# A two-layer diffusion backbone kernel: strides of 4192 and 4176 bytes for the weight slots, moving rows on multiples of 2048 bytes

## The chip, the core and the metric

The kernel runs on one core of a Trainium2 chip. The metric is device time in microseconds (us). TensorE (PE in the rows) multiplies, its weight loads have rows of their own (PEld), VectorE is DVE, ScalarE is ACT, GpSimd is POOL, and SyncE (SP) issues most of the DMAs. Times of single instructions are in nanoseconds (ns) where marked.

## What is computed

Two layers over 256 latent tokens and 256 context tokens, D_MODEL 1024, D_FF 2816, everything in float32. Cut to what matters:

```
for l in range(DEPTH):                                   # DEPTH = 2
    h  = h  + 0.5*m[2]*_swiglu(_modulate(_rms(h,  norm_w[l,0]), m[0], m[1]), ffn1_w_gu[l], ffn1_w_down[l])
    hc = hc + 0.5*mc[2]*_swiglu(...)                     # the same for the context
    u, uc = _modulate(_rms(h, norm_w[l,1]), ...), _modulate(_rms(hc, norm_w[l,1]), ...)
    y, yc = _hybrid_mixer(u, uc, ...)                    # differential attention | gated conv | pools, w_in, w_out
    h  = h + m[5]*y
    h  = h + 0.5*m[8]*_swiglu(_modulate(_rms(h, norm_w[l,2]), m[6], m[7]), ffn2_w_gu[l], ffn2_w_down[l])
    ...                                                  # the context too, except in the last layer
return h
```

m and mc are nine modulation vectors, silu(c) @ w_mod[l] + b_mod[l]. The weight matrices make up nearly all of the traffic and of the multiplications.

## The kernel before

**Three products for one.** The activations stand transposed in SBUF: 1024 features as 8 chunks of 128 partitions, 512 columns of tokens (the latent tokens first, then the context). Each float32 product x·w is made from a high and a low half of both: hi_w·hi_x + hi_w·lo_x + lo_w·hi_x. The helper `three` (lines 1167 to 1170) issues these as three float32r matmuls into one PSUM bank: L1168 has the weights' high half (whi) and the activations' high half, L1169 whi and the activations' low half, L1170 the weights' low half (wlo) and the activations' high half. Each matmul has its own weight load of 128 columns. The moving operand is a row of xh, xl (the layer's input) or ah, al (the hidden values of a feed-forward network) with 512 columns, 2048 bytes in a partition, or a half of such a row with 256 columns. In the value blocks of the mixer alone (192 matmuls) it is the other way round: the weights move and the activations are loaded.

**The weight stream.** The weights come in 320 blocks (NB) of 128 x 1024 float32, 8 tiles of 128 x 128, in the order of use. SP issues the DMA of block n into `raw[:, n % RING]`, RING = 5, when block n - 5 has been used (block_done). ACT copies it rounded into `whi[:, n % SPL]`, SPL = 4 (`split`, L398), when block n - 4 has been used. DVE subtracts: `wlo[:, n % RING] = raw - whi` (L685). wlo and raw are the same memory: the low half overwrites the raw block. PE waits for lo_done of block n, and the last matmul of a block counts block_done up. All queues are written out by hand; no scheduler orders them.

**Around it.** While the first feed-forward networks run, DVE also makes the modulation of later stages (L706, L710), a multiply-add of 128x512 at a time from `wm`, and PE sums it with small matmuls (L1229). The statistics of the norms (L1244, L1246, L1331), attention scores (L1371), values (L1403) and transposes are plain float32 matmuls, between the blocks.

**The layout.** Every SBUF tensor is placed behind the one allocated before it, on a multiple of 32 bytes. The first one starts at byte 16512 of each partition. The `hidden` and `wm0_place` stacks share the place of kq and what follows it. With the tensors' sizes this gives, for the ones that the float32r matmuls read:

```
tensor     starts at   start modulo 2048   step from slot to slot (or row to row)
wlo, raw   16512       128                 4096
whi        36992       128                 4096
xh         69760       128                 2048
xl         86144       128                 2048
ah         137344      128                 2048
al         182400      128                 2048
```

A tile of 128 weight columns has 512 bytes, so before the change every start address of a float32r matmul, weights or moving row, is 128 above a multiple of 512. A moving row of 512 columns runs from 128 to 2176 above a multiple of 2048; of its halves, the first runs from 128 to 1152 and the second from 1152 to 2176.

Of the kernel before, what the change touches and what calls it, by code (L numbers as in the profile page):

```python
# [22 lines left out]
F32, F32R = mybir.dt.float32, mybir.dt.float32r  # L23
# [3 lines left out]
P = 128  # L27
D = 1024
DC = D // P
S = 256  # L30
T = 2 * S
DEPTH = 2
# [11 lines left out]
TILES = 8  # L44
BLK = TILES * P
RING = 5
SPL = 4
GU = 2 * FC
DN = FC
HALF = DN // 2  # L50
# [6 lines left out]
TAIL_CHUNKS = (6, 7, 4, 5, 0, 1, 2, 3)  # L57
FFN = GU + DN
MIX = VB + QKB + CB + OB
# [4 lines left out]
HN = D // 2  # L64
# [5 lines left out]
START_UNITS = 4  # L70
UNIT_AT = {0: (4, GU // 4), 1: (16, GU // 4), 2: (27, 9)}
LATE_UNIT = 15
# [22 lines left out]
NCOL = _at  # L95
# [4 lines left out]
def program(nc, wstream, wmod, cols, x_t, out):  # L100
    with ExitStack() as ctx:
        def sb(name, shape, dt=F32):
            return ctx.enter_context(nc.sbuf_tensor(name, shape, dt))
# [2 lines left out]
            return ctx.enter_context(nc.semaphore(name))  # L106


        ring = ExitStack()
        raw = ring.enter_context(nc.sbuf_tensor("raw", [P, RING, BLK], F32))  # L110
        ring.close()
        wlo = sb("wlo", [P, RING, TILES, P], F32R)
        whi = sb("whi", [P, SPL, TILES, P], F32R)
        h = sb("h", [P, DC, T])
        xh = sb("xh", [P, DC, T], F32R)
        xl = sb("xl", [P, DC, T], F32R)
        xh32 = xh[:, :, :].bitcast(F32)
        wm = sb("wm", [P, 2, 2, HN])
        K = sb("K", [P, NCOL])
        cs = sb("cs", [P, DC * 2])  # L120
        modc = sb("modc", [P, DEPTH * N_MOD, DC, 2])
        acol = sb("acol", [P, DEPTH * 3, DC, 2])
        gcol = sb("gcol", [P, DEPTH * 3, DC, 2])
        lamc = sb("lamc", [P, DEPTH, 8])
        qws = sb("qws", [P, 16])
        mrows = sb("mrows", [P, P])

        shared_a = sb("shared_a", [P, 3 * T])
        macc = shared_a[:, 0:2 * HN].rearrange("p (v n) -> p v n", v=2)
        sq = shared_a[:, 0:2 * T].rearrange("p (a t) -> p a t", a=2)  # L130
        ssq = shared_a[:, 2 * T:3 * T]

        shared_b = sb("shared_b", [P, 4 * T])
        sil = shared_b[:, 0:2 * T].rearrange("p (a t) -> p a t", a=2)
        af = shared_b[:, 2 * T:4 * T].rearrange("p (a t) -> p a t", a=2)
        lnv = shared_b[:, 0:T]
        rstd = shared_b[:, T:2 * T]
        xt = shared_b[:, 2 * T:4 * T].rearrange("p (a t) -> p a t", a=4)
        hidden = ExitStack()
        ah = hidden.enter_context(nc.sbuf_tensor("ah", [P, FC * T], F32R))  # L140
        al = hidden.enter_context(nc.sbuf_tensor("al", [P, FC * T], F32R))
# [10 lines left out]
        sqk = sb("sqk", [P, 2, T])  # L152
        lnk = sb("lnk", [P, T])
        rq = sb("rq", [P, 2, T])
        shf = sb("shf", [P, S])
        rot = sb("rot", [P, S])
        prob = sb("prob", [P, 2, 2, T])
        att = sb("att", [P, 3, T])
# [7 lines left out]
        lsum = sb("lsum", [P, 2, 2, 2])  # L166
        linv = sb("linv", [P, 2, 2, 2])
        nlin = sb("nlin", [P, 2, 2])
        ps = ctx.enter_context(nc.psum_tensor("ps", [P, 8, T], F32))

        def col(name, i=0, n=1):
            a = COLS[name][0] + i
            assert i + n <= COLS[name][1]
            return K[:, a:a + n]

# [142 lines left out]
        @block.sync  # L318
        def _(sp):
            sp.dma_start(K[:, 0:EARLY], cols[:, 0:EARLY]).then_inc(cols_in, 16)  # L320
            sp.dma_start(h[:, :, :], x_t.rearrange("(c p) t -> p c t", p=P)).then_inc(x_in, 16)
            start_pairs = wmod[0:START_UNITS * PAIRS].rearrange("(u q) p n -> q p u n", q=PAIRS)
            for p in range(PAIRS - 1):
                sp.dma_start(wm0[:, p, :, :, :].rearrange("p u a n -> p u (a n)"), start_pairs[p])\  # L324
                    .then_inc(wm0_in[p], 16)
            for r in range(2):

                sp.dma_start(wm0[:, PAIRS - 1, :, r, :], start_pairs[PAIRS - 1][:, :, r * HN:(r + 1) * HN])\  # L328
                    .then_inc(wm0_in[PAIRS - 1 + r], 16)
            for n in range(NB):  # L330
                if n >= RING:

                    sp.wait_ge(block_done, n - RING + 1)
                sp.dma_start(raw[:, n % RING, :], wstream[n]).then_inc(raw_in[n % RING], 16)
                if n == 1:
                    sp.dma_start(K[:, EARLY:NCOL], cols[:, EARLY:NCOL]).then_inc(cols2_in, 16)
                    sp.dma_start(lamk[:, :], cols[:, NCOL:NCOL + NLAM]).then_inc(lam_in, 16)
            for d in range(DC):

                sp.wait_ge(h_done, h_count(5, d, 0))  # L340
                sp.dma_start(out[d * P:(d + 1) * P, :], h[:, d, 0:S]).then_inc(out_sem, 16)
            sp.wait_ge(out_sem, 16 * DC)
# [48 lines left out]
        def _(act):  # L391
            def split(n):

                act.wait_ge(raw_in[n % RING], 16 * (n // RING + 1))
                if n >= SPL:

                    act.wait_ge(block_done, n - SPL + 1)
                act.activation(whi[:, n % SPL, :, :].rearrange("p a b -> p (a b)"), raw[:, n % RING, :], ACT.Copy)\  # L398
                    .then_inc(hi_done, 1)

            def split_next(n):
                if n + SPL < NB:
                    split(n + SPL)

# [13 lines left out]
            def ffn(l, st):  # L418
# [11 lines left out]
                for b in range(HALF):  # L430
                    split_next(n0 + GU + b)
                if m + 1 < 6:
                    for d in range(JOINT):
                        square(m + 1, d)
                    ln_exp_tables()
                nd = n0 + GU + HALF
                for b in range(HALF - TAIL):
# [7 lines left out]
            def ln_exp_tables():  # L445

                act.preload_act_table_set("natural_log_exp_and_others")
# [225 lines left out]
        def _(dve):  # L673
            steps = [0]

            def own(ins):

                steps[0] += 1
                ins.then_inc(dve_step, 1)
                dve.wait_ge(dve_step, steps[0])  # L680
# [8 lines left out]
            def split_next(n):  # L689
                if n + SPL < NB:  # L690
                    split(n + SPL)
# [154 lines left out]
            def ffn(l, st):  # L846
# [8 lines left out]
                def mods(b):  # L855

                    i, e = divmod(b - LAG, PAIRS)
                    if 0 <= i < nu:
                        mod_pair(u0 + i, e)
# [10 lines left out]

                nd = n0 + GU
                for b in range(HALF - 1):
                    split_next(nd + b)
                    mods(GU + b)
                    if nu and b == ROWS_AT[f]:
# [30 lines left out]
            def conv_sum(l, c):  # L906
# [7 lines left out]
                own(dve.tensor_tensor(u[:, :, 1:S + 1], sv(c), sv(2 + c), ALU.mult))  # L914
                own(dve.tensor_scalar(y, u[:, :, 1:S + 1], K[:, cw + 1:cw + 2], None, ALU.mult))
                own(dve.scalar_tensor_tensor(y, u[:, :, 0:S], K[:, cw:cw + 1], y, ALU.mult, ALU.add))
                own(dve.scalar_tensor_tensor(y, u[:, :, 2:S + 2], K[:, cw + 2:cw + 3], y, ALU.mult, ALU.add))

# [692 lines left out]
```

## Time and profile before

| | us |
|---|---|
| median of 3 runs | 1715.92 (1715.57 to 1716.11) |
| the profiled execution | 1716.46 |
| its span, first to last instruction | 1714.7 |
| granted clock of TensorE, mean | 0.993 |
| 512-column matmuls of `three` | 4836 |
| 256-column matmuls of `three` | 3624 |

The profiled execution lies 0.5 us above the median. How to read the views: in "lines" a group is one line, engine, operation and shape, with its busy time, the mean of one, and the idle time before it. A matmul's duration holds its way through the array and overlaps the next one, so what a matmul costs is the distance from its start to the start of the next, and the timeline shows that. PEclk, or the clock, is the share of TensorE's full 2.4 GHz that was granted: 1.00 is 2.4 GHz, 0.50 is 1.2 GHz. In the chain of work that ended last each step is followed back to what released it.

### The profile page before, as it was taken

How to read it: one execution, taken by the hardware profiler on the slowest of the kernel's cores; microseconds unless marked ns; L12 is line 12 of the kernel's file. 1: busy time of each engine (PE TensorE's matmuls, PEld its weight loads, DVE VectorE, ACT ScalarE, POOL GpSimd, SP SyncE). 2: the span in 40 equal slices, each digit the busy share in tenths (PEclk: the TensorE clock that was granted, in tenths of full speed). 3: DMA queues.
4: the chain of work that ended last, by engine and by line, in shares of the span. 5: the costliest groups of instructions: out<-in, count | busy, mean ns of one | idle time of the engine just before them, and what ended most of it. 6: DMA issues, size and time to landing. Idle time of an engine off the chain costs nothing.

```text
span 1714.7 us, 23714 instructions
## 1 busy us (share of the span) xinstructions
PE 1664.4 (97%) x9475; PEld 1412.5 (82%) x9475; DVE 1085.4 (63%) x1652; ACT 609.5 (36%) x917; POOL 85.0 (5%) x150
## 2 busy tenths in 40 slices
PE   3999999999999999999999999999999999979999
PEld 1888888889767898888888898888888987979999
DVE  2777787636668567777773368777523587655543
ACT  2422222124645452222222252222222365444432
POOL 0000000000000100000000000000000000000000
PEclk9999999999999999999999999999999999989999
DMA  9255555532211224555552235555323232435554
GB/s 365 96 187 190 180 195 179 191 111 75 99 62 50 87 87 163 183 195 179 190 188 97 83 101 195 183 185 187 134 97 98 87 111 74 139 116 182 183 169 148
DMA packets 69882, 249.42 MB, mean 145 GB/s; under 512 B 7441, under 2 KB 8465, under 8 KB 69777
## 3 DMA queue, kind: packets, MB, share of 16 engines
q1 hardware_dynamic: 51344, 180.83, 31.7%
q0 software_dynamic: 18432, 67.12, 11.7%
q8 instruction: 75, 1.23, 0.3%
q14 instruction: 31, 0.25, 0.0%
HBM read 246.87 MB, written 1.05 MB: 145 GB/s over the span
## 4 chain that ended last, share of the span: by engine, by line
PE 93%; DVE 2%; DMA 1%; SPq 1%; issue 1%; ACT 1%; POOLq 0%; POOL 0%; DVEq 0%; ACTq 0%
PE ps L1168 30%; PE ps L1169 29%; PE ps L1170 29%; DMA raw<-wstream 1%; PE ps L1229 1%; PE ps L1371 1%; PE ps L1403 1%; ACT whi L398 1%; PE ps L1331 1%; DVE wlo L685 1%; SPq L328 1%; SPq L324 0%; PE ps L1385 0%; DVE nmax L1013 0%; PE ps L1412 0%
## 5 line engine op out<-in xcount | busy, mean ns | idle before, releaser
L685 DVE TENSOR_TENSOR wlo<-raw,whi 128x1024 fp32r<-128x1024 f32 x320 | 393.7, 1230 | 546.8 <-ACT whi L398 545.9
L1168 PE MATMUL ps<-xh,whi 128*128 128x512 f32 (+1 forms) x1956 | 690.2, 353 | 8.5 <-DVE xl L795 5.1
L1169 PE MATMUL ps<-xl,whi 128*128 128x512 f32 (+1 forms) x1956 | 674.3, 345 | 0.0
L1170 PE MATMUL ps<-xh,wlo 128*128 128x512 f32 (+1 forms) x1956 | 673.7, 344 | 0.0
L398 ACT ACTIVATE whi<-raw 128x1024 fp32r<-128x1024 f32 x320 | 338.6, 1058 | 897.5 <-PE ps L1170 764.2
L1168 PEld LDWEIGHTS ps<-xh,whi 128*128 128x128 f32 x1956 | 372.3, 190 | 65.7 <-issue 12.0
L1169 PEld LDWEIGHTS ps<-xl,whi 128*128 128x128 f32 x1956 | 372.6, 190 | 45.7 <-issue 3.8
L1170 PEld LDWEIGHTS ps<-xh,wlo 128*128 128x128 f32 x1956 | 372.2, 190 | 44.7
L710 DVE SCALAR_TENSOR_TENSOR shared_a<-wm,cs,shared_a 128x512 f32<-128x512 f32 x448 | 307.6, 747 | 0.0
L1168 PE MATMUL ps<-ah,whi 128*128 128x512 f32 (+1 forms) x800 | 274.9, 344 | 3.7 <-DVE shared_b L733 3.7
L1169 PE MATMUL ps<-al,whi 128*128 128x512 f32 (+1 forms) x800 | 273.0, 341 | 0.0
L1170 PE MATMUL ps<-ah,wlo 128*128 128x512 f32 (+1 forms) x800 | 272.9, 341 | 0.0
L1168 PEld LDWEIGHTS ps<-ah,whi 128*128 128x128 f32 x800 | 152.4, 190 | 23.2 <-DVE shared_b L733 5.2
L1170 PEld LDWEIGHTS ps<-ah,wlo 128*128 128x128 f32 x800 | 152.4, 190 | 17.0
L1169 PEld LDWEIGHTS ps<-al,whi 128*128 128x128 f32 x800 | 152.5, 191 | 16.8
L356 POOL DMA_DIRECT2D wm<-wmod x126 | 66.8, 530 | 912.2 <-DVEq L713 904.6
L463 ACT ACTIVATE shared_a<-h 128x256 f32<-128x256 f32 (+1 forms) x64 | 31.6, 498 | 82.2 <-DVE h L752 73.4
L752 DVE SCALAR_TENSOR_TENSOR h<-ps,gcol,h 128x256 f32<-128x256 f32 x104 | 45.7, 478 | 20.9 <-PE ps L1170 20.9
L733 DVE TENSOR_TENSOR shared_b<-shared_b,ps 128x512 f32<-128x512 f32 (+1 forms) x88 | 54.1, 615 | 2.5 <-ACT shared_b L411 2.5
L740 DVE TENSOR_TENSOR al<-shared_b,ah 128x512 fp32r<-128x512 f32 (+1 forms) x88 | 54.5, 619 | 1.5 <-ACT ah L416 1.2
L479 ACT ACTIVATE xh<-shared_b,modc 128x256 fp32r<-128x256 f32 x88 | 42.2, 504 | 31.0 <-DVE shared_b L787 31.0
L416 ACT ACTIVATE ah<-shared_b 128x512 fp32r<-128x512 f32 (+1 forms) x88 | 49.5, 562 | 5.6 <-DVE shared_b L733 5.6
(106 smaller groups left out, 797.5 us busy)
## 6 DMA issues: line engine op xcount, KB each, us to landing
raw<-wstream SPq DMA_DIRECT2D x320, 512.0 KB, 3.5
wm<-wmod POOLq DMA_DIRECT2D x128, 512.0 KB, 4.7
wm<-wmod SPq DMA_DIRECT2D x3, 2048.0 KB, 21.0
h<-x_t SPq DMA_DIRECT2D x1, 2048.0 KB, 11.9
wm<-wmod SPq DMA_DIRECT2D x2, 1024.0 KB, 20.4
out_t<-h SPq DMA_DIRECT2D x8, 128.0 KB, 2.6
K<-cols SPq DMA_DIRECT2D x1, 939.0 KB, 13.8
K<-cols SPq DMA_DIRECT2D x1, 268.5 KB, 3.0
```

The lines of the kernel that those rows point to most:

```text
L356: pool.dma_start(wm[:, c, :, :].rearrange("p a n -> p (a n)"), wmod[bass.ds(i * 2 + c, 1)].rearrange("a p n -> p (a n)"))\
L398: act.activation(whi[:, n % SPL, :, :].rearrange("p a b -> p (a b)"), raw[:, n % RING, :], ACT.Copy)\
L416: act.activation(ah[:, j * T:j * T + w], af[:, j % 2, 0:w], ACT.Copy).then_inc(ah_done, 1)
L479: act.activation(xh[:, d, s * S:(s + 1) * S], xt[:, (g - 1) % 4, :], ACT.Identity, bias=modc[:, N_MOD * l + 3 * st, d, s:s + 1]).then_inc( ...
L685: dve.tensor_tensor(wlo[:, n % RING, :, :].rearrange("p a b -> p (a b)"), raw[:, n % RING, :], whi[:, n % SPL, :, :].rearrange("p a b -> p ...
L710: ins = dve.scalar_tensor_tensor(acc, src, sc, acc, ALU.mult, ALU.add)
L733: dve.tensor_tensor(af[:, j % 2, 0:w], sil[:, j % 2, 0:w], ps[:, gu_bank(f, 2 * j + 1), 0:w], ALU.mult)\
L740: dve.tensor_tensor(al[:, dst], af[:, j % 2, 0:w], ah[:, dst].bitcast(F32), ALU.subtract)\
L752: ins = dve.scalar_tensor_tensor(h[:, d, v * S:(v + 1) * S], ps[:, bank, v * S:(v + 1) * S], gcol[:, m, d, v:v + 1], h[:, d, v * S:(v + 1) ...
L1168: pe.matmul(out_ap, hi_w, hi_x, start=start, stop=False)
L1169: pe.matmul(out_ap, hi_w, lo_x, start=False, stop=False)
L1170: return pe.matmul(out_ap, lo_w, hi_x, start=False, stop=stop)
```

## The change

Four things change in the allocations, and nothing else. (1) A slot of raw/wlo gets 24 float32 of padding (LO_SLOT, 4192 bytes), a slot of whi 20 (HI_SLOT, 4176 bytes); the code still reads and writes the first 1024 of each. (2) modc, acol, gcol and the tensors of the mixer and of the hidden values move to the front. (3) A tensor `fill` of 608 bytes, used by nobody, brings xh, and with it xl and h, to a multiple of 2048. ah and al are on multiples of 2048 too. (4) shf moves to the end. The order of the instructions of every engine, their shapes, waits and counts stay the same; only the addresses and the line numbers (3 higher) differ.

```diff
--- before.py
+++ after.py
@@ -45,6 +45,8 @@
 BLK = TILES * P
 RING = 5
 SPL = 4
+LO_SLOT = BLK + 24
+HI_SLOT = BLK + 20
 GU = 2 * FC
 DN = FC
 HALF = DN // 2
@@ -106,36 +108,9 @@
             return ctx.enter_context(nc.semaphore(name))
 
 
-        ring = ExitStack()
-        raw = ring.enter_context(nc.sbuf_tensor("raw", [P, RING, BLK], F32))
-        ring.close()
-        wlo = sb("wlo", [P, RING, TILES, P], F32R)
-        whi = sb("whi", [P, SPL, TILES, P], F32R)
-        h = sb("h", [P, DC, T])
-        xh = sb("xh", [P, DC, T], F32R)
-        xl = sb("xl", [P, DC, T], F32R)
-        xh32 = xh[:, :, :].bitcast(F32)
-        wm = sb("wm", [P, 2, 2, HN])
-        K = sb("K", [P, NCOL])
-        cs = sb("cs", [P, DC * 2])
         modc = sb("modc", [P, DEPTH * N_MOD, DC, 2])
         acol = sb("acol", [P, DEPTH * 3, DC, 2])
         gcol = sb("gcol", [P, DEPTH * 3, DC, 2])
-        lamc = sb("lamc", [P, DEPTH, 8])
-        qws = sb("qws", [P, 16])
-        mrows = sb("mrows", [P, P])
-
-        shared_a = sb("shared_a", [P, 3 * T])
-        macc = shared_a[:, 0:2 * HN].rearrange("p (v n) -> p v n", v=2)
-        sq = shared_a[:, 0:2 * T].rearrange("p (a t) -> p a t", a=2)
-        ssq = shared_a[:, 2 * T:3 * T]
-
-        shared_b = sb("shared_b", [P, 4 * T])
-        sil = shared_b[:, 0:2 * T].rearrange("p (a t) -> p a t", a=2)
-        af = shared_b[:, 2 * T:4 * T].rearrange("p (a t) -> p a t", a=2)
-        lnv = shared_b[:, 0:T]
-        rstd = shared_b[:, T:2 * T]
-        xt = shared_b[:, 2 * T:4 * T].rearrange("p (a t) -> p a t", a=4)
         hidden = ExitStack()
         ah = hidden.enter_context(nc.sbuf_tensor("ah", [P, FC * T], F32R))
         al = hidden.enter_context(nc.sbuf_tensor("al", [P, FC * T], F32R))
@@ -152,7 +127,6 @@
         sqk = sb("sqk", [P, 2, T])
         lnk = sb("lnk", [P, T])
         rq = sb("rq", [P, 2, T])
-        shf = sb("shf", [P, S])
         rot = sb("rot", [P, S])
         prob = sb("prob", [P, 2, 2, T])
         att = sb("att", [P, 3, T])
@@ -166,6 +140,35 @@
         lsum = sb("lsum", [P, 2, 2, 2])
         linv = sb("linv", [P, 2, 2, 2])
         nlin = sb("nlin", [P, 2, 2])
+        fill = sb("fill", [P, 152])
+        xh = sb("xh", [P, DC, T], F32R)
+        xl = sb("xl", [P, DC, T], F32R)
+        xh32 = xh[:, :, :].bitcast(F32)
+        h = sb("h", [P, DC, T])
+        ring = ExitStack()
+        raw = ring.enter_context(nc.sbuf_tensor("raw", [P, RING, LO_SLOT], F32))[:, :, 0:BLK]
+        ring.close()
+        wlo = sb("wlo", [P, RING, LO_SLOT], F32R)[:, :, 0:BLK].rearrange("p s (a b) -> p s a b", b=P)
+        whi = sb("whi", [P, SPL, HI_SLOT], F32R)[:, :, 0:BLK].rearrange("p s (a b) -> p s a b", b=P)
+        wm = sb("wm", [P, 2, 2, HN])
+        K = sb("K", [P, NCOL])
+        cs = sb("cs", [P, DC * 2])
+        lamc = sb("lamc", [P, DEPTH, 8])
+        qws = sb("qws", [P, 16])
+        mrows = sb("mrows", [P, P])
+
+        shared_a = sb("shared_a", [P, 3 * T])
+        macc = shared_a[:, 0:2 * HN].rearrange("p (v n) -> p v n", v=2)
+        sq = shared_a[:, 0:2 * T].rearrange("p (a t) -> p a t", a=2)
+        ssq = shared_a[:, 2 * T:3 * T]
+
+        shared_b = sb("shared_b", [P, 4 * T])
+        sil = shared_b[:, 0:2 * T].rearrange("p (a t) -> p a t", a=2)
+        af = shared_b[:, 2 * T:4 * T].rearrange("p (a t) -> p a t", a=2)
+        lnv = shared_b[:, 0:T]
+        rstd = shared_b[:, T:2 * T]
+        xt = shared_b[:, 2 * T:4 * T].rearrange("p (a t) -> p a t", a=4)
+        shf = sb("shf", [P, S])
         ps = ctx.enter_context(nc.psum_tensor("ps", [P, 8, T], F32))
 
         def col(name, i=0, n=1):
```

The same table after the change:

```
tensor     starts at   start modulo 2048   step
wlo, raw   157696      0                   4192: the 5 slots at 0, 96, 192, 288, 384 modulo 512
whi        178656      480                 4176: the 4 slots at 480, 48, 128, 208 modulo 512
xh         108544      0                   2048
xl         124928      0                   2048
ah         18432       0                   2048
al         63488       0                   2048
```

All slots still start on a multiple of 16 bytes. Slots 1 and 3 of raw/wlo start at 32 above a multiple of 64, the others on one; slots 1 and 3 of whi start at an odd multiple of 16. A 512-column moving row of xh, xl, ah or al now begins and ends on a multiple of 2048.

## Rows read from the trace of the kernel before

**Rows 1.** the page, parts 1 and 2: busy us by engine; granted clock.
```profile
PE 1664.4 (97%) x9475; PEld 1412.5 (82%) x9475; DVE 1085.4 (63%) x1652; ACT 609.5 (36%) x917; POOL 85.0 (5%) x150
...
PEclk9999999999999999999999999999999999989999
```

**Rows 2.** the page, part 4: shares of the chain that ended last, by engine.
```profile
PE 93%; DVE 2%; DMA 1%; SPq 1%; issue 1%; ACT 1%; POOLq 0%; POOL 0%; DVEq 0%; ACTq 0%
```

**Rows 3.** lines by shape: xcount | busy us, mean ns | idle before us.
```profile
L1168 PE MATMUL ps<-xh,whi 128*128 128x512 f32 x1116 | 443.8, 398 | 0.6 <-issue 0.6
...
L1168 PE MATMUL ps<-xh,whi 128*128 128x256 f32 x840 | 246.4, 293 | 7.8 <-DVE xl L795 5.1 <-POOL xl L377 1.7 <-DVE shared_b L733 0.9
...
L1168 PE MATMUL ps<-ah,whi 128*128 128x512 f32 x432 | 169.4, 392 | 1.3 <-DVE shared_b L733 1.3
...
L1168 PE MATMUL ps<-ah,whi 128*128 128x256 f32 x368 | 105.5, 287 | 2.4 <-DVE shared_b L733 2.4
...
L1168 PE MATMUL ps<-whi,xh 128*128 128x512 f32 x64 | 26.5, 415 | 0.0
```

**Rows 4.** timeline of PE, 512-column matmuls: start us, duration us.
```profile
99.31 0.39 PE L1170 MATMUL ps<-xh,wlo 128*128 128x512 f32 x1
...
117.67 0.39 PE L1170 MATMUL ps<-xh,wlo 128*128 128x512 f32 x1
```

**Rows 5.** timeline of PE, 256-column matmuls, first halves of the rows.
```profile
393.74 0.28 PE L1168 MATMUL ps<-ah,whi 128*128 128x256 f32 x1
...
403.58 0.28 PE L1169 MATMUL ps<-al,whi 128*128 128x256 f32 x1
```

**Rows 6.** timeline of PE, 256-column matmuls, second halves of the rows.
```profile
411.02 0.28 PE L1170 MATMUL ps<-ah,wlo 128*128 128x256 f32 x1
...
416.30 0.28 PE L1169 MATMUL ps<-al,whi 128*128 128x256 f32 x1
```

**Rows 7.** timeline of PE, 256-column matmuls; clock in the next group.
```profile
1514.40 0.41 PE L1170 MATMUL ps<-xh,wlo 128*128 128x256 f32 x1
...
1519.52 0.41 PE L1170 MATMUL ps<-xh,wlo 128*128 128x256 f32 x1
```

**Rows 8.** stretches: us; busy of PE, PEld, DVE, ACT, POOL; PEclk, DMA, GB/s.
```profile
1514.00:1519.00 5.00, 5.00 (x24) 5.00 (x25) 4.50 (x12) 2.54 (x5) 0.00 (x0) 0.50 0.01 3
99.00:117.00 18.00, 18.00 (x82) 14.88 (x81) 13.66 (x19) 4.88 (x7) 1.59 (x3) 1.00 0.52 179
53.00:290.00 237.00, 237.00 (x1189) 193.81 (x1189) 179.30 (x258) 69.49 (x90) 20.14 (x38) 1.00 0.53 178
1470.00:1715.00 245.00, 226.49 (x1824) 223.82 (x1822) 126.55 (x170) 101.35 (x144) 4.21 (x4) 0.96 0.50 160
```

**Rows 9.** the chain by time: start us, us; 512-column plain float32 passes.
```profile
442.06 1.72 PE ps L1331 x4
```

**Rows 10.** by line, L685 and L398: ns min/median/max, first and last start.
```profile
L685 DVE TENSOR_TENSOR wlo<-raw,whi x320: 1215/1226/2316, 36.4 to 1703.0; 128x1024 fp32r<-128x1024 f32 x160
L398 ACT ACTIVATE whi<-raw x320: 1039/1060/1082, 35.3 to 1701.9; 128x1024 fp32r<-128x1024 f32 x160
```

**Rows 11.** timeline of PE behind a group of small matmuls (L1229).
```profile
119.14 0.40 PE L1170 MATMUL ps<-xh,wlo 128*128 128x512 f32 x1
...
121.00 0.39 PE L1169 MATMUL ps<-xl,whi 128*128 128x512 f32 x1
```

**Rows 12.** landings of raw; waits: us in total, times, longest us.
```profile
DMA to landing us min/median/max: 3.3/3.5/15.6
ACT whi L398 <- DMA raw<-wstream: 133.2, 68, 16.3
```

**Rows 13.** the chain in order of time, 1625 to 1660 us.
```profile
1641.70 3.98 DMA raw<-wstream
...
1648.02 0.34 DVE shared_b L733
```

## The prediction

> **What bounds the kernel now.** I read the page first. TensorE is busy for 1664.4 us, 97% of the span, at full clock in nearly all slices [rows 1], and the chain that ended last is 93% PE [rows 2]. So only two things can move the time: what a matmul costs, or a gap in PE's stream. The lines by shape give the counts [rows 3]: three products each of 1116 + 432 + 64 matmuls with 512 columns, 4836, and of 840 + 368 with 256 columns, 3624, together 8460. The idle time before them is a few us in all, so gaps hardly exist.
>
> What one costs is the distance between starts. With 512 columns, 81 steps take from 99.31 to 117.67 us [rows 4]: 226.7 ns. With 256 columns, 82 steps take from 393.74 to 403.58 us: 120.0 ns [rows 5]. At 2.4 GHz, 512 columns are 213.3 ns and 256 columns are 106.7 ns. Both shapes thus pay the same 13.3 ns, 32 clock cycles, beyond their columns. The reader should see next that this is not always so: where the clock is granted at 0.50, as from 1514 to 1519 us [rows 8], 24 steps take from 1514.40 to 1519.52 us, 213.3 ns [rows 7], which is exactly 256 columns at 1.2 GHz and nothing on top. The plain float32 matmuls, with as many weight loads, take 1.72 us for four passes of 512 columns [rows 9], 430 ns each: two cycles a column (426.7) and 3 ns. So the 13.3 ns appear only where the moving row is read at one column per cycle of the full clock. They are a price of reading weights and row together.
>
> Check of the sum: 4836 x 226.7 ns + 3624 x 120.0 ns = 1096.3 + 434.9 = 1531 us, 89% of the span. The extra 13.3 ns make 8460 x 13.3 = 113 us of it. That is all that a layout could win on PE.
>
> **The change, part by part.** No instruction is added, removed or moved, on no queue, DMAs and waits included. Only addresses change, so each part is worth what an access costs at another address.
>
> (a) Moving rows on multiples of 2048. Before, the second halves of the rows cross a multiple of 2048 and the first halves do not. The first halves step at 120.0 ns [rows 5]; the second halves, 44 steps from 411.02 to 416.30 us, at 120.0 ns too [rows 6]. Crossing costs nothing, so its removal gives nothing: 0 us.
>
> (b) Padded weight slots as PE reads them. Before, weights and moving row always stand at the same place modulo 512, while their distance modulo 2048 goes through all four multiples of 512 as the tile index runs (and the row's half changes it again). In the 81 steps of rows 4 and the 82 of rows 5 all of these distances occur, and the step stays the same. So distances by multiples of 512 do not matter. Distances within 512 bytes are not in the trace at all: there the change goes from one value to nine (0 to 480). The bounds are 0 ns left of the 13.3, 113 us gained, and on the other side at least one more such price, 8460 x 13.3 = 113 us lost. Which value do I take? The nearest rows are those of (a) and of rows 4 and 5, in which every address variation that exists leaves the step alone, and 32 cycles are the same for both row lengths, which fits a load that takes the same time wherever it lies. I take 0, and keep both ends for the range.
>
> By the Trainium skill (SBUF — State Buffer, Who interferes with whom) PE has two independent read ports, one for the moving operand and one for the weight load, and never waits on anyone; TensorE: Matmul & The Clock Gate (Wait — 56ns, not 53.3ns?) gives a 512-column step of bf16 as 215.7 ns. By that rule the 226.7 ns of rows 4 would hold 11 ns too many for each matmul, something that a layout might return; this trace disagrees with the rule as it stands. [...]
>
> (c) Padded slots as ACT and DVE use them. ACT's rounding takes 1039 to 1082 ns over 320 blocks, DVE's subtraction has a median of 1226 ns against a least of 1215 [rows 10]. In all 320 they run beside PE, DMAs and each other, in five slots against four and at ever other moments of each other, and hardly spread. So there is no collision between engines that different strides could cure: 0. If they became dearer, cover is there: between 99 and 117 us, where DVE is fullest, it is busy 13.66 of 18 us [rows 8]. A 512-column block takes 24 x 226.7 = 5.44 us, of which DVE has 24% free, 1.3 us. Its one subtraction a block could double (1.23 to 2.46 us) before DVE becomes the bound there.
>
> (d) The DMAs into the padded slots. A raw block lands 3.5 us after its issue [rows 12]. It is issued five blocks ahead; with 256 columns a block is 24 x 120 = 2.88 us, so four blocks give 11.5 us for 3.5 + 1.06 + 1.23 = 5.8 us. ACT's 133.2 us of waiting for raw cost PE nothing then, as it runs ahead. Once in the tail they do: the chain goes from 1641.70 us through a DMA of 3.98 us to DVE's 0.34 us at 1648.02 [rows 13]. If each landing became 1 us longer at the new addresses, an assumed size, I would lose about 1 us there and little elsewhere (PE is busy 226.5 of 245 us from 1470 us on [rows 8], and most of the rest is the norm before the last network, without a block to wait for). I take 0, ends -1 and +3 us.
>
> (e) K, wm, h, shared_a and the rest at new places. The plain float32 passes show 3 ns beyond their columns [rows 9], so there is little to win, 1015 x 3 ns = 3 us for all that are not in `three`, 9475 less 8460 [rows 1, 3]; at the worst they lose 13.3 ns each, 13.5 us. I take 0, the row's own price.
>
> The sum is 0: a profiled execution of 1716.46 us stays there, with a span of 1714.7 us; the runs' median is 0.5 us lower, so the forecast is 1715.9 us.
>
> **The rivals.** *The load's reads collide by address (faster).* Half clock and plain float32 [rows 7, 9] show that the 13.3 ns vanish when the row is read at half the rate, so it is contention, and before, all 8460 pairs stand on one value modulo 512. If only that value collides, what remains is the first low-half slot, a fifth of a third of the matmuls: the gain is 113 x 14/15 = 105 us, 1611 us. If reads meet in part of the new distances, I take half: 53 us, 1663 us. Against it: a price that is 32 cycles without any spread, in both lengths, looks fixed.
>
> *The shifted slots cost PE more (slower).* The same contention could be at its mildest with everything on one grid, and slots that lie off the old grid could cost a load further cycles. Place: every load from a shifted slot in `three`. It decides from 3.4 us on, 0.2% of the time, which is 0.41 ns a matmul, one cycle more for each load. The nearest dearer rows are the 8 steps from 119.14 to 121.00 us behind a group of small matmuls, 232.5 ns, 6 ns more [rows 11]: at all matmuls that is 51 us, 1767 us. If only the two whi slots at odd multiples of 16 bytes pay 13.3 ns more, it is half of two thirds of 8460, 2820 x 13.3 = 37 us, 1753 us. I take 1753. Against it stands the same lack of spread.
>
> *ACT, DVE or DMA become dearer, and it stays hidden.* Same time as the forecast, by (c) and (d).
>
> **How the numbers follow.** A measurement of this kernel tells about 0.2% (3.4 us) from no change. No effect of the addresses on PE, with all that stays hidden: 0.50, at 1715.9, own range 1712.5 to 1719.3. Faster by collisions that end: 0.30; of this about 0.18 for gains up to 70 us, 0.12 beyond. Slower by dearer loads: 0.20, of which 0.14 up to 40 us, 0.06 beyond. To hold 8 in 10, I reach to 1645 below and 1755 above, which leaves 0.12 and 0.06 out. Most of the doubt is about one thing that the trace of before cannot show, the distances within 512 bytes.
>
> **What will show each step.** In the timeline of PE the steps with 512 and 256 columns: 226.7 and 120.0 ns if I am right; 213 to 226 ns, differing from slot to slot, if the first rival holds; above 227 ns, in blocks whose number leaves 1 or 3 when divided by four, if the second does. The first and second halves of the rows must step alike (a). ACT's 1060 and DVE's 1226 ns should stay (c), and so should the landing of 3.5 us (d). The forecast is wrong if a step of PE changes by more than 0.4 ns on the mean, or if a new wait stands before L1171 to L1173.

## The result and the profile after

The changed kernel takes 1729.81 us (1728.54 to 1731.27, 4 runs) against 1715.77 us (1715.57 to 1716.11) for the kernel before: a ratio of 1.0082, 95% interval 1.0069 to 1.0095. It is slower by 0.8%, 14.0 us, where no change was forecast. The profiled execution took 1731.27 us with a span of 1729.5 us, 14.8 us more than before, at the same mean clock of 0.993.

The page after, parts 1, 2 and 4 (before: [rows 1, 2]):

```profile
PE 1679.1 (97%) x9475; PEld 1405.4 (81%) x9475; DVE 1085.3 (63%) x1652; ACT 609.7 (35%) x917; POOL 84.6 (5%) x150
...
PEclk9999999999999999999999999999999999989999
...
PE 92%; DVE 2%; DMA 2%; ACT 1%; issue 1%; SPq 1%; POOLq 0%; POOL 0%; DVEq 0%; ACTq 0%
```

PE is busy 14.7 us longer, and idle for 50.4 us against 50.3: no wait was added, the matmuls themselves got dearer. DVE and ACT did not. By line (ns min/median/max, first and last start), and the landing of raw, after:

```profile
L688 DVE TENSOR_TENSOR wlo<-raw,whi x320: 1211/1225/2320, 35.3 to 1718.4; 128x1024 fp32r<-128x1024 f32 x160
...
L401 ACT ACTIVATE whi<-raw x320: 1039/1060/1082, 34.3 to 1717.3; 128x1024 fp32r<-128x1024 f32 x160
```

```profile
DMA to landing us min/median/max: 3.3/3.5/14.9
```

All three stand as in [rows 10, 12]. What changed is the distance between starts. The timeline of PE after, 512 columns and then 256 (start us, duration us):

```profile
98.92 0.40 PE L1172 MATMUL ps<-xl,whi 128*128 128x512 f32 x1
...
117.97 0.40 PE L1173 MATMUL ps<-xh,wlo 128*128 128x512 f32 x1
```

```profile
1559.80 0.28 PE L1171 MATMUL ps<-xh,whi 128*128 128x256 f32 x1
...
1579.91 0.29 PE L1173 MATMUL ps<-xh,wlo 128*128 128x256 f32 x1
```

82 steps in 19.05 us are 232.3 ns, where [rows 4] has 226.7. 170 steps in 20.11 us are 118.3 ns, where [rows 5] has 120.0. **The two shapes went opposite ways.** Before, nearly every step was alike; now they alternate, as in this stretch of the timeline after:

```profile
713.65 0.39 PE L1171 MATMUL ps<-xh,whi 128*128 128x512 f32 x1
713.88 0.39 PE L1172 MATMUL ps<-xl,whi 128*128 128x512 f32 x1
714.11 0.39 PE L1173 MATMUL ps<-xh,wlo 128*128 128x512 f32 x1
714.34 0.40 PE L1171 MATMUL ps<-xh,whi 128*128 128x512 f32 x1
714.57 0.40 PE L1172 MATMUL ps<-xl,whi 128*128 128x512 f32 x1
714.81 0.39 PE L1173 MATMUL ps<-xh,wlo 128*128 128x512 f32 x1
715.04 0.39 PE L1171 MATMUL ps<-xh,whi 128*128 128x512 f32 x1
715.26 0.39 PE L1172 MATMUL ps<-xl,whi 128*128 128x512 f32 x1
715.49 0.39 PE L1173 MATMUL ps<-xh,wlo 128*128 128x512 f32 x1
```

At a finer unit of time than these rows print, a run of such steps reads 225, 230, 229, 231, 234, 238 ns and repeats. Over all steps without a wait and at full clock, the mean with 512 columns went from 227.29 to 232.19 ns, that with 256 columns from 119.84 to 118.00. The sum: 4836 x 4.90 = +23.7 us, 3624 x 1.84 = -6.7 us, together +17.0, against 14.8 us of span (the steps at half clock and behind waits, which these means leave out, are part of the rest). All 20 pairs of a whi slot with a wlo slot are dearer with 512 columns: in the first network three steps take 693 to 703 ns, before 680 to 686. With 256 columns, in the last network, 18 pairs are cheaper (350 to 357 ns, before 360). The two pairs of whi's slot at 128 modulo 512 with wlo's slots at 96 and 192 stay, at 360.0 and 358.8 ns.

At half clock the 256-column step did not change. Where the granted clock is 0.50, 11 steps with 256 columns take 2.35 us after the change, 213.6 ns, and [rows 7] has 213.3:

```profile
1534.90 0.41 PE L1171 MATMUL ps<-xh,whi 128*128 128x256 f32 x1
...
1537.25 0.41 PE L1173 MATMUL ps<-xh,wlo 128*128 128x256 f32 x1
```

### The profile page after: what moved, and what is told of

Read it like the earlier page. It is cut to its first block, busy times and chain, and to the rows that moved or that the text cites. A ratio compares the mean times of both kernels' runs of the same rounds, so it can differ in the third digit from the quotient of the medians.

```text
span 1729.5 us, 23714 instructions
## 1 busy us (share of the span) xinstructions
PE 1679.1 (97%) x9475; PEld 1405.4 (81%) x9475; DVE 1085.3 (63%) x1652; ACT 609.7 (35%) x917; POOL 84.6 (5%) x150
## 4 chain that ended last, share of the span: by engine, by line
PE 92%; DVE 2%; DMA 2%; ACT 1%; issue 1%; SPq 1%; POOLq 0%; POOL 0%; DVEq 0%; ACTq 0%
PE ps L1171 30%; PE ps L1172 29%; PE ps L1173 29%; DMA raw<-wstream 2%; PE ps L1232 1%; PE ps L1374 1%; ACT whi L401 1%; PE ps L1406 1%; PE ps L1334 1%; DVE wlo L688 1%; SPq L331 1%; PE ps L1388 0%; SPq L327 0%; DVE nmax L1016 0%; PE ps L1415 0%
## 5 line engine op out<-in xcount | busy, mean ns | idle before, releaser
L736 DVE TENSOR_TENSOR shared_b<-shared_b,ps 128x512 f32<-128x512 f32 (+1 forms) x88 | 54.1, 614 | 2.5 <-ACT shared_b L414 2.5
```

Of the source, the lines that this page charges most:

```text
L736: dve.tensor_tensor(af[:, j % 2, 0:w], sil[:, j % 2, 0:w], ps[:, gu_bank(f, 2 * j + 1), 0:w], ALU.mult)\
```

## The experiments

In all of them "distance" is the start of the weights minus the start of the moving row, in bytes.

**Which part of the change costs: alignment or padding?** Theory A: the padding, by its distances within 512 bytes. Theory B: the rows on multiples of 2048, or the tensors moved. The first kernel is the changed one without padding:

```diff
-LO_SLOT = BLK + 24
-HI_SLOT = BLK + 20
+LO_SLOT = BLK
+HI_SLOT = BLK
```

> The changed kernel without the padding: slots 4096 bytes apart, everything else where the change puts it, so that weights and moving rows all start on multiples of 512 and the rows on multiples of 2048. Theory A (the distance between a weight tile and the moving row within 512 bytes sets the step of a matmul): the distance is 0 again for all, steps of 226.7 and 120.0 ns, time 1716 us. Theory B (the rows on multiples of 2048 are what costs): the steps and the time of the changed kernel, 1730 us.

Measured: 1715.35 us (1713.21 to 1716.01, 10 runs), ratio 0.9995 (0.9986 to 1.0005). The mean steps are 227.33 and 119.85 ns. Rows on multiples of 2048 and moved tensors change nothing. The second is the kernel before, its order of tensors kept, with the padded slots alone (rows 128 above a multiple of 1024):

```diff
+LO_SLOT = BLK + 24
+HI_SLOT = BLK + 20
...
-        wlo = sb("wlo", [P, RING, TILES, P], F32R)
-        whi = sb("whi", [P, SPL, TILES, P], F32R)
+        wlo = sb("wlo", [P, RING, LO_SLOT], F32R)[:, :, 0:BLK].rearrange("p s (a b) -> p s a b", b=P)
+        whi = sb("whi", [P, SPL, HI_SLOT], F32R)[:, :, 0:BLK].rearrange("p s (a b) -> p s a b", b=P)
+        fill = sb("fill", [P, 56])
```

The slots of raw, the same memory as wlo, are padded with it.

> The kernel before with the padded slots alone: order of the tensors as before, moving rows 128 above a multiple of 1024, and a filler of 224 bytes so that the distances of the slots to the rows modulo 512 are those of the changed kernel (0, 96, 192, 288, 384 for the low halves, 480, 48, 128, 208 for the high ones). Theory A: the time of the changed kernel, 1729 to 1731 us, with mean steps near 232 and 118 ns. Theory B: 1716 us.

Measured: 1732.45 us (1730.16 to 1736.67), ratio 1.0101 (1.0081 to 1.0121), steps 232.18 and 118.03 ns. Two stretches of PE show it in the counts of matmuls that run in them. The rows are, in this order, of before, of the kernel without padding, and of the one with padding alone (us, PE busy (x matmuls), PEclk, DMA share, GB/s):

```profile
99.00:117.00 18.00, 18.00 (x82) 1.00 0.52 179
1560.00:1580.00 20.00, 20.00 (x169) 1.00 0.58 182
```

```profile
99.00:117.00 18.00, 18.00 (x81) 1.00 0.54 179
1560.00:1580.00 20.00, 20.00 (x169) 1.00 0.56 181
```

```profile
99.00:117.00 18.00, 18.00 (x79) 1.00 0.54 183
1560.00:1580.00 20.00, 20.00 (x171) 1.00 0.57 184
```

82 or 81 against 79 with 512 columns, 169 against 171 with 256. Theory A holds, B falls: the rows and tensors stand elsewhere than in the changed kernel, and only the distances are the same.

**Is it PE alone?** Theory C: the padded slots collide with what ACT, DVE and the DMAs do meanwhile. A probe runs PE alone, after everything is loaded: blocks of 24 matmuls as in `three`, at chosen places. The block, shortened:

```
def block_of(hi, lo, row, w):            # places in float32, w columns
    for c in range(8):
        h = whi[:, hi + c * P:hi + (c + 1) * P]
        l = wlo[:, lo + c * P:lo + (c + 1) * P]
        r = slice(row + c * T, row + c * T + w)
        matmul(h, xh[:, r]); matmul(h, xl[:, r]); matmul(l, xh[:, r])
```

> A probe that leaves the whole computation out: PE alone runs blocks of 24 matmuls in the order of `three` (high weights with a high row, high weights with a low row, low weights with a high row), with 512 and with 256 columns, with nothing beside it on ACT, DVE or the DMAs. 33 distances of both weight tiles to the row in steps of 16 bytes (0 to 512); ten other starts of the row; the 20 pairs of slots of the changed kernel; distances of 4, 8 and 12 bytes. Theory A: 680 ns for three 512-column matmuls and 360 ns for three 256-column ones at distance 0, and for the 20 pairs 693 to 702 and 351 to 357 ns as in the changed kernel. Theory C (the padded slots collide with reads and writes of ACT, DVE and DMAs): 680 and 360 ns everywhere, since none of these works here.

The timeline of the probe's PE at distance 0 (L71 to L73 are the three matmuls), 512 and 256 columns, then the same at distance 16:

```profile
48.45 0.39 PE L71 MATMUL ps<-xh,whi 128*128 128x512 f32 x1
...
53.43 0.39 PE L72 MATMUL ps<-xl,whi 128*128 128x512 f32 x1
53.89 0.28 PE L71 MATMUL ps<-xh,whi 128*128 128x256 f32 x1
...
56.52 0.28 PE L72 MATMUL ps<-xl,whi 128*128 128x256 f32 x1
```

```profile
56.99 0.40 PE L72 MATMUL ps<-xl,whi 128*128 128x512 f32 x1
...
62.12 0.39 PE L73 MATMUL ps<-xh,wlo 128*128 128x512 f32 x1
62.36 0.28 PE L71 MATMUL ps<-xh,whi 128*128 128x256 f32 x1
...
64.96 0.28 PE L72 MATMUL ps<-xl,whi 128*128 128x256 f32 x1
```

Each has 22 steps between its first and last row: 226.4 and 119.5 ns, then 233.2 and 118.2. At a finer unit, by distance:

```
distance      0    16    32    64    96   128   144   160   192   208   240   256
512 columns 226.7 233.3 233.3 233.3 234.3 232.0 226.7 233.3 229.0 233.3 228.4 226.7
256 columns 120.0 118.4 118.3 117.8 118.4 118.4 119.4 120.0 117.8 116.7 120.0 120.0
```

From 256 on the values repeat. The 20 pairs of slots of the change took 231.0 to 234.1 and 116.9 to 120.0 ns with no other engine at work, like the changed kernel's 232.19 and 118.00. The two pairs at 120.0 ns are the two that stayed near 360 ns for three steps in the kernel. Theory C falls: **with PE alone, the step depends on where the weights lie relative to the moving row.**

**Where is the best place?** The second probe puts the row at 16 places of 16 bytes each, and the weights at 16, with both lengths.

```diff
+            def set_plane():
+                for r in range(16):
+                    for w in range(16):
+                        block_of(w * LINE, w * LINE, r * LINE, T)
+                        block_of(w * LINE, w * LINE, r * LINE, S)
```

> The probe again, PE alone, computation left out: 16 starts of the row times 16 starts of the weight tiles, both in steps of 16 bytes from 0 to 240, each with a block of 24 matmuls of 512 columns and one of 256. Theory A1 (only the distance modulo 256 counts): all pairs with the same distance have the same steps, 226.7 and 120.0 ns on the diagonal. Theory A2 (the place of the row within 256 bytes counts too): steps differ along a diagonal; the first probe had 226.7 ns at 0 and 0 but 231.1 ns at 16 and 16, and 113.3 ns for 256 columns with the row at 64 and the weights at 0 against 117.8 ns with the row at 0 and the weights at 192.

The steps depend on the distance modulo 256 and on whether the row stands on an even or an odd multiple of 16. With 512 columns they go from 226.7 ns (even rows: distances 0 and 144; odd rows: 32 and 192) to 240.0 (odd rows, 96); with 256 from 113.3 (odd rows: 64, 192 and mostly 240) to about 120. Distance 0 has its 226.7 and 120.0 ns on even rows alone; on odd rows it has 231.1 and 118.3. Six of the 512 readings lie 2 to 13 ns off the others of their distance and kind of row: with the row at 176, distance 96 took 226.7 ns, not 240.0. So the rule has exceptions even with PE alone. Lowest in both are odd rows with the weights at distance 192, 64 below the row modulo 256. Here the row at 80 with the weights at 16 (18 steps each):

```profile
727.77 0.39 PE L73 MATMUL ps<-xh,wlo 128*128 128x512 f32 x1
...
731.85 0.39 PE L73 MATMUL ps<-xh,wlo 128*128 128x512 f32 x1
```

```profile
732.99 0.28 PE L73 MATMUL ps<-xh,wlo 128*128 128x256 f32 x1
...
735.04 0.28 PE L73 MATMUL ps<-xh,wlo 128*128 128x256 f32 x1
```

**Does a probe's step hold in the kernel?** First a place that the probe gave as a little dear with 512 columns (228.9 ns) and cheap with 256 (113.3): the row 64 above the weights, on an even multiple of 16. The second probe gave 117.8 ns with 256 columns for that place, so even with PE alone one place has had two steps.

```diff
+        fill_w = sb("fill_w", [P, 32])
         ring = ExitStack()
...
+        fill_x = sb("fill_x", [P, 16])
         h = sb("h", [P, DC, T])
```

> The kernel before with two fillers and no padding of slots: weights on multiples of 256, moving rows 64 above one. The first probe had, for this pair, steps of 113.3 ns with 256 columns and 228.9 ns with 512. If the kernel follows the probe: 3624 x -6.67 = -24.2 us and 4836 x +2.22 = +10.7 us, 1702 us. If the probe, with nothing beside PE, does not carry over to the kernel, or only the distance counts (117.8 and 229.0 ns, as with the row at 0 and the weights at 192): -8.0 and +11.1 us, 1719 us.

Measured: 1717.01 us (1713.31 to 1719.34, 10 runs), ratio 1.0008 (0.9999 to 1.0018); steps 229.18 and 116.05 ns. The second is a mean of two: some stretches run at 117.8 ns a step and others, 970 steps of the last network among them, at 113.3, the values of the two probes. One shape's gain about pays for the other's loss. Next the best place: rows at 208, weights at 144 modulo 256.

```diff
+OFF = 4
+FX = 8
+FA = 56
...
-        wlo = sb("wlo", [P, RING, TILES, P], F32R)
-        whi = sb("whi", [P, SPL, TILES, P], F32R)
+        w_all = sb("w_all", [P, (RING + SPL) * BLK + 8], F32R)
+        wlo = w_all[:, OFF:OFF + RING * BLK].rearrange("p (s a b) -> p s a b", a=TILES, b=P)
...
+        fill_x = sb("fill_x", [P, FX])
+        x_all = sb("x_all", [P, 2 * DC * T + 8], F32R)
...
+        fill_a = sb("fill_a", [P, FA])
...
+        a_all = hidden.enter_context(nc.sbuf_tensor("a_all", [P, 2 * FC * T + 8], F32R))
```

whi, xh, xl, ah and al are slices of these three tensors in the same way, and raw starts at OFF too.

> The kernel before with all weight slots 4096 bytes apart on 144 modulo 256 and all moving rows of xh, xl, ah and al on 208 modulo 256: the row starts on an odd multiple of 16 bytes and the weights 64 bytes below it (192 above, modulo 256). The plane of the second probe has 226.7 ns with 512 columns and 113.3 ns with 256 there, and the same in four other places on that diagonal. Theory A2 (distance modulo 256 and the row's place modulo 32 set the step): 3624 x -6.67 = -24.2 us, and about +1 us for the 192 matmuls with the roles exchanged: 1692 us. If only the distance counted, as in the third experiment: 1713 to 1719 us. If the kernel's other engines disturb the pattern: between the two.

Measured: **1703.48 us (1701.06 to 1707.21, 6 runs), ratio 0.9933 (0.992 to 0.9946): 12 us faster than the kernel before, 26 us faster than the changed one.** With 512 columns the step is 226.97 ns, with 256 the mean is 116.69, where the probe had 113.3: half of the 24 us that were expected came. In its timeline the last network runs at two step lengths. These are 170 steps of 118.4 ns, and further on 178 of 113.4, at the same places modulo 256:

```profile
1599.81 0.28 PE L1177 MATMUL ps<-x_all,w_all 128*128 128x256 f32 x1
...
1619.93 0.28 PE L1179 MATMUL ps<-x_all,w_all 128*128 128x256 f32 x1
```

```profile
1659.77 0.28 PE L1177 MATMUL ps<-a_all,w_all 128*128 128x256 f32 x1
...
1679.95 0.28 PE L1178 MATMUL ps<-a_all,w_all 128*128 128x256 f32 x1
```

None of the 28 uninterrupted stretches of at least 20 such steps changes its length on the way. The length changes only where something comes between: a wait, or other matmuls with no idle time, as the norm's between 405 and 407 us.

**Do the slots act one by one?** If each load had a price of its own, two thirds of the effect should come with whi's padding and one third with wlo's. Theory M: the three loads and the rows form one pattern, so that it does not divide. The changed kernel with one of the paddings:

```diff
-HI_SLOT = BLK + 20
+HI_SLOT = BLK
...
+        fill_h = sb("fill_h", [P, 8])
         whi = sb("whi", [P, SPL, HI_SLOT], F32R)[:, :, 0:BLK].rearrange("p s (a b) -> p s a b", b=P)
```

> The changed kernel with the low halves' slots padded (4192) and the high halves' slots 4096 apart on multiples of 256. Theory L (each load costs by its own distance to the row beside it): a third of the loads is off the grid, so only the steps beside a low half's load change, about +6 ns with 512 columns and -2 with 256, and the time is a third of the way, 1720 to 1721 us. Theory M (a load off the grid shifts the next ones too, the order of the three being one pattern): the steps beside the high halves' loads, whose distance is 0, move away from 226.7 and 120.0 ns too, and the time is nearer to the changed kernel's, 1724 to 1732 us.

```diff
-LO_SLOT = BLK + 24
+LO_SLOT = BLK
...
+        fill_h = sb("fill_h", [P, 56])
         whi = sb("whi", [P, SPL, HI_SLOT], F32R)[:, :, 0:BLK].rearrange("p s (a b) -> p s a b", b=P)
```

> The other half of the padding: the high halves' slots padded (4176) at their places of the changed kernel, the low halves' on distance 0. Theory L: two thirds of the way, 1725 us, with the steps beside a low half's load at 226.7 and 120.0 ns. Theory M: those steps move too, 1727 to 1733 us.

Measured: wlo padded alone 1728.14 us (1725.7 to 1729.94), ratio 1.0075 (1.0058 to 1.0092); whi alone 1733.41 us (1732.52 to 1734.83), 1.0105 (1.0088 to 1.0122). The first gives nearly all of the loss, not a third, the second more than all of it. In the first, with whi at distance 0 as before, the mean steps with 512 columns by line are 230.69, 231.80 and 230.34 ns, all higher than the 227.3 of before. Theory M holds.

A third probe placed whi and wlo apart from each other, then xl apart from xh, then the weights on steps of 4 bytes, with the row at 80.

```diff
+                for hi in range(16):
+                    for lo in range(16):
+                        block_of(hi * LINE, lo * LINE, 20, T)
+                        block_of(hi * LINE, lo * LINE, 20, S)
...
+                for w in range(64):
+                    block_of(w, w, 20, T)
+                    block_of(w, w, 20, S)
```

> The probe with the row at 80 (an odd multiple of 16), computation left out: first 16 x 16 places of the high weights' tile and the low weights' tile, each on its own; then 16 x 16 places of both weights together and of the low half's row alone; then 64 places of the weights in steps of 4 bytes. If each load meets the row that runs beside it and nothing else, the least steps stay 226.7 and 113.3 ns wherever the others lie; if a better pair exists, it shows below these, down to 213.3 and 106.7 ns.

Nothing was below 226.7 and 113.3 ns; both at once came with all weights at 16. Most others lay at 228 to 236 and 117 to 120. One place for the weights on a multiple of 8 bytes, 40, gave 226.7 and 113.8, and was tried in the kernel:

```diff
-FX = 8
+WOFF = 10
+FX = 0
...
-        w_all = sb("w_all", [P, (RING + SPL) * BLK + 8], F32R)
-        wlo = w_all[:, OFF:OFF + RING * BLK].rearrange("p (s a b) -> p s a b", a=TILES, b=P)
+        w_all = sb("w_all", [P, (RING + SPL) * BLK + 16], F32R)
+        wlo = w_all[:, WOFF:WOFF + RING * BLK].rearrange("p (s a b) -> p s a b", a=TILES, b=P)
```

> As the version with the row on 208 and the weights on 144 modulo 256, but with the weights on 168, 40 bytes below the row. The third probe had 226.7 and 113.8 ns there. That version kept the 226.7 ns for 512 columns but fell into 118 ns for most 256-column matmuls, with 113.3 in the rest, and each lasted from one gap of PE to the next. If the lower state is easier to hit from this distance: down to 1693 us. If the states mix as before: 1700 to 1707 us.

Measured: 1722.07 us (1721.19 to 1724.91), ratio 1.0038 (1.0024 to 1.0052). The 256-column steps are 113.66 ns all through, but the 512-column ones 232.17, not the probe's 226.7, so both expectations were missed. In its two stretches 79 and 179 matmuls run:

```profile
99.00:117.00 18.00, 18.00 (x79) 1.00 0.53 183
1560.00:1580.00 20.00, 20.00 (x179) 1.00 0.60 195
```

So a step of the probe, in which both lengths take turns every 24 matmuls and no other engine works, is no promise for the kernel. Which of the two differences matters was not tried.

**What sets the length in the last network?** The rows of the last feed-forward network are moved by 58 float32 to place 184, the rest is the kernel of 1703.48 us:

```diff
+TAIL_SHIFT = 58
...
+def moved(m):
+    return TAIL_SHIFT if m == 5 else 0
...
-                                xh[:, c, a:b], xl[:, c, a:b], c == 0, c == DC - 1)
+                                xh[:, c, a + k:b + k], xl[:, c, a + k:b + k], c == 0, c == DC - 1)
```

> The version with rows on 208 and weights on 144 modulo 256, and in the last feed-forward network alone, where all 1584 matmuls of `three` have 256 columns, the rows start 232 bytes further, on 184: the 40 bytes above the weights at which the 256-column steps were 113.4 ns all through. Expected if the place of the row sets the step stage by stage: about 1056 matmuls of that stage go from 118.3 to 113.4 ns, 5 us less than the version without the shift, 1696 to 1701 us. If the steps are a matter of what PE did before and not of the place, the same time as that version, 1701 to 1707 us.

Measured: 1708.9 us (1707.35 to 1709.69), ratio 0.996 (0.9946 to 0.9974). The last network ran at 120.0 ns a step all through (169 matmuls from 1560 to 1580 us, as before the change): both expectations were missed. The weights lie 40 bytes below the row here as in the kernel of 1722.07 us, whose steps took 113.66 ns with the row at 208, so the distance alone does not set the length. The row's own place can be what differs, as in the second probe, or what PE did before; these runs do not tell them apart. Then the kernel with rows at 208 and weights at 144 again, unchanged:

> The version with rows on 208 and weights on 144 once more, beside the one with the shifted tail: 1701 to 1707 us as before.

Measured: 1705.48 us (1702.94 to 1707.81), ratio 0.9946 (0.9932 to 0.9959). Its last network does it the other way round, 178 steps of 113.3 ns in the first stretch and 170 of 118.4 in the second:

```profile
1599.75 0.28 PE L1179 MATMUL ps<-x_all,w_all 128*128 128x256 f32 x1
...
1619.92 0.28 PE L1177 MATMUL ps<-x_all,w_all 128*128 128x256 f32 x1
```

```profile
1659.80 0.28 PE L1178 MATMUL ps<-a_all,w_all 128*128 128x256 f32 x1
...
1679.92 0.28 PE L1177 MATMUL ps<-a_all,w_all 128*128 128x256 f32 x1
```

The same program at the same places has several step lengths, and something at an interruption chooses. What that is stays open.

**The steps account for the times.** For each kernel: the mean steps without waits, what they give against before (4836 and 3624 matmuls), by how much the span of that same execution differs from the 1714.7 us of before, and what the median of all runs moved by (ratio less 1, times 1716 us):

```
kernel                    512 col.  256 col.  by steps, us  its span, us  all runs, us
before                     227.29    119.84
changed kernel             232.19    118.00      +17.0         +14.8         +14.1
without padding            227.33    119.85       +0.2          -0.4          -0.9
padding alone              232.18    118.03      +17.1         +16.7         +17.3
rows at 64                 229.18    116.05       -4.6          -3.1          +1.4
rows 208, weights 144      226.97    116.69      -13.0         -12.0         -11.5
the same again             226.95    115.81      -16.2         -13.5          -9.3
wlo padded alone           230.96    118.65      +13.4          +9.3         +12.9
whi padded alone           232.45    118.17      +18.9         +16.0         +18.0
rows 208, weights 168      232.17    113.66       +1.2          +6.3          +6.5
last network at 184        226.96    118.13       -7.8          -6.9          -6.9
```

Steps and spans agree within 3 us in eight of the ten. With wlo padded alone the span is 4.1 us less than the steps say; there PE was busy at half clock for 11.5 us, against 16.0 before. With the weights at 168 it is 5.1 us more, and 3.8 of them are idle time of PE (54.1 us against 50.3). The medians lie up to 4.5 us from the span of the one execution. The 256-column length differs between executions, as the repeat shows, and may be the reason; that is not shown, as each run has one trace.

## Why the prediction was wrong

*The number.* 1729.81 us lies outside the 1712.5 to 1719.3 us that the forecast gave to "no effect", and in the slower case, which had a chance of 0.20.

*What bounds the kernel*: right. PE's steps set the time, and the loss is all in PE's busy time (+14.7 of +14.8 us of span).

*Part (a), rows on multiples of 2048, 0 us*: right, and shown by the kernel without padding (0.9995).

*Part (b), padded slots as PE reads them, taken as 0*: **this is the step that failed.** The prediction said itself that the distances within 512 bytes are not in the trace, and then took the value of the nearest rows, [rows 4 to 6], where distances by multiples of 512 leave the step alone. That was no evidence for smaller ones. The probe shows why: the step repeats every 256 bytes, so every distance that occurred before was the same place of the period, and the constant step was one sample of the curve, not 163. The second ground, that 13.3 ns in both lengths without any spread look like a fixed load, fell with it: that equality belongs to distance 0 with the row on an even multiple of 16. Elsewhere a step costs 6.7 ns (113.3 with 256 columns) to 26.7 ns (240.0 with 512) beyond its columns. The size of the term was +17.0 us where 0 was taken, inside the bounds of -113 and +113 us, which were far too wide. The least that any place gave was 226.7 and 113.3 ns together, 3624 x 6.7 = 24 us, not 113.

The prediction weighed a rule of the Trainium skill here: SBUF — State Buffer (Who interferes with whom) has PE's two read ports independent and PE waiting on no one. The measurements differ: the probe, with PE alone, goes from 226.7 to 240.0 ns by address alone. A fixed price of each load does not fit either, as the steps hold from 16 cycles beyond the columns (113.3 ns) to 64 (240.0 ns).

*Part (c), ACT and DVE, 0 us*: right (1060 and 1225 ns). *Part (d), landings, 0 us*: right (3.5 us). *Part (e), 0 us*: right within what the kernel without padding can tell.

*The rivals.* The faster one (collisions by address that end) was right that the time beyond the columns depends on the address, and that it is gone at half clock (213.6 ns after the change too); it was wrong in where the padding leads: the old common distance 0 was, with 512 columns, already at the least of the curve. The slower one had the direction and the mechanism's kind, but not its place. It laid the price on the two whi slots at odd multiples of 16 bytes, 13.3 ns each, 1753 us. Measured was +4.90 ns on the mean of the 4836 matmuls with 512 columns, with every pair of slots dearer, and -1.84 ns on that of the 3624 with 256, which the prediction did not have at all: it held one price for both shapes. Its own deciding point, 0.41 ns a matmul, was passed: the mean is (23.7 - 6.7) / 8460 = 2.0 ns.

*What would show it.* The forecast was to be wrong if a mean step moved by over 0.4 ns, and it moved. The sign for the slower rival, blocks that leave 1 or 3 when divided by four, did not show: with 512 columns all 20 pairs of slots are dearer, with 256 18 of them are cheaper.

## What to carry to other kernels

A quantity that is constant over all rows of a trace says nothing about an address that the program never varied: count how many different values, modulo a small power of two, the rows really hold before you take their value for a new one. Where float32r matmuls with a weight load each set the time at full clock, these runs speak for weights and moving rows on one place modulo 256 bytes that is an even multiple of 16 (the step before the change) or, better here by 0.7 and 0.5%, rows on an odd multiple of 16 with all weights 64 bytes below. Slots staggered by 80 and 96 bytes cost 0.8%. Measure a layout in the kernel itself, as a probe with short blocks gave a step that the kernel did not keep.

## What the runs showed of the hardware

- With PE alone, the step of a float32r matmul with its own weight load depends on the distance between weights and moving row modulo 256 bytes, and on the row's place modulo 32: 226.7 to 240.0 ns with 512 columns, 113.3 to about 120 with 256. The best place of one length is mostly not that of the other.
- At half clock the address did not matter: 213.3 ns with 256 columns before, 213.6 ns after the change.
- It is a pattern over several matmuls, not a price of each load: padding wlo alone also lengthened the steps of whi's matmuls, from 227.3 to 230.7 and 231.8 ns.
- One program at one layout has two step lengths with 256 columns, 113.3 and 118.4 ns (with the rows 64 above the weights 113.3 and 117.8), and the last network with its rows shifted to 184 ran at a third, 120.0. They change only where a wait or other matmuls interrupt, and are not the same ones in each execution. Why the steps take these values, and what picks one after a gap, these runs leave open.
